# Four edits to a two-block transformer kernel: conv filling, PSUM rings, a fifth feed-forward weight buffer, and the place of weight splits in layer 1

## The chip, the cores and the metric

The kernel runs on one core of a Trainium2 chip. The metric is the device time of one execution in microseconds (us). Before the change three runs took 1944.5 to 1952.13 us, with a median of 1948.22.

## What is computed

Two model blocks follow each other, all in float32, with 256 latent tokens and 256 context tokens of width 1024. The first block has two layers:

```
layer 0: h += g1 * (concat(conv, neighbourhood attention) @ w_out)
         conv = gb * dwconv3(gc * u)          # gb, gc, u: columns of a @ w_in
         h += g2 * ((silu(n @ w1) * (n @ w3)) @ w2)    # D_FF = 2816
         the same for the context tokens
layer 1: window attention and differential attention, w_out
         mixture of 8 experts, top 2
```

The gates g1, g2 and the shifts and scales of the norms are `silu(c) @ ada_w + ada_b`. The second block has a dilated attention and a latent attention (q and kv go through norms of rank 512 and 256 and are projected up by `w_uq` and `w_ukv`), two sigmoid gates of 1024 columns each, `w_out`, and an MLP with squared ReLU.

## The kernel before

Every product of float32 data is made of three matmuls. An operand is split in a high part (rounded to the matmul's fp32r format) and a low part (what is left). Weights come from HBM in tiles of at most 128 x 2048 values (1 MB). A tile lands in the raw half of a buffer ("slot"). ScalarE writes the high part (line 1464, `whi`), then VectorE writes the low part over the raw values (line 1976, `wlo`). In the text this is the split. Then TensorE uses the tile (`mm3`, lines 889 to 891). In the trace each slot has three names: raw60, wlo61, whi62 for slot 0; raw64, wlo65, whi66 for slot 1; raw68, wlo69, whi70 for slot 2; raw137, wlo138, whi139 for the feed-forward's own slot. A smaller part of the slots' use is modulation: tiles of `ada_w` are not split but multiplied on VectorE with silu(c) and summed (line 2009, `wsum`), four instructions for two modulation vectors, two for one.

The order is fixed ahead. The five engines' programs are run once in Python to count semaphores and to lay out the tiles (`TILES`). `use` and `sums` give each tile the slot that has been out of use longest, from `open_slots`, or from `state["loads"]` and `state["adds"]` where these are set. SyncE issues the loads in one order and waits, for each, until the slot's previous tile is used up or summed. A modulation tile is loaded just after the weight tile that follows it. ScalarE and VectorE are strict in order as well. They call `feed(event)` ahead of nearly every operation. It splits all tiles up to the one in use at that event plus `at["ahead"]` (counted in tiles, modulation tiles too), and stops at a tile whose slot is still in use at that event. `feed` on VectorE also adds the sums that are owed.

PSUM has eight banks. `take(ring, ...)` goes around a list of banks (`RINGS`) and waits until the bank's last holder has been read. Rings "8", "4", "x", "c" are banks 0 to 7, 0 to 3, 0 to 3, and 4 and 5.

The places that the change touches, in the order of the run:

- Layer 0's attention ("a0", 32 units, from 157 us). Each step of the loop computes a unit's scores; the transposes and the product with V follow three and four units later. In between, TensorE works on a generator, here the 12 conv feature products (8 steps each of three matmuls; 96 steps in all). `FILLED[i]` says how many steps are done after unit i, `CONV_AT` in which unit each product ends, and ScalarE and VectorE take the results up in `convolved(i)`. 16 steps (the products c and u of the first feature group) are done before the attention, ahead of the transposes of the keys.
- Layer 0's feed-forward (366 to 766 us). Two blocks of 11 hidden tiles: 12 weight tiles of `w1` and `w3` by turns (48 matmuls each, the last two of a block 24), then `w2` in two halves of 3 tiles (48, 48 and 36 matmuls). 28 modulation tiles run beside them, one after each weight tile. The very last half goes token by token and so needs its three tiles at once. The results are multiplied by the gate on VectorE (line 2284) and added on GpSimd.
- Around the second block's last two halves ScalarE issues 13 small loads for layer 1 (lines 1667 to 1676), VectorE makes the rotation tables (`tables`, lines 2407 to 2416), and ScalarE then takes an exponential (line 1679).
- Layer 1: norm "o", projections cq (2 tiles) and ckv (1), then the pair tiles dq0, dq1, dk0, ..., and attention "a1" from 831 us.
- Second block: the last projections are the latents; their transposes, then the first products of the gates (two banks of eight, ahead of attention "a2"), then "a2" from 1557 us, and the products `uq` and `ukv` after it.

Of the kernel before, what the change touches and what calls it, by code (L numbers as in the profile page):

```python
# [280 lines left out]
def _build(nc, ctx, I, cst_d, scr_d, out_d, packed):  # L281
# [88 lines left out]
    HIDf = v3(LF.pair(11 * 512), 11)  # L370
    SILf, THDf = LF.some(3, 512), LF.some(3, 512)
    slot_f = slot(LF.col)
    LF.col += 4096
    slot_f_end = LF.col
    TMPf = LF.some(4, 512)
# [425 lines left out]
    FILLED = [16 + (i + 1) * 80 // 28 if i < 27 else 96 for i in range(40)]  # L801
    CONV_AT = {f: min(i for i in range(-1, 40) if ([16] + FILLED)[i + 1] >= 8 * (n + 1)) for n, f in enumerate(FEATS)}
    HEADS["a0"].filled = FILLED
    HEADS["a2"].filled = [min(64, 18 + 2 * i) for i in range(40)]
    GATE_AT = {(n, t): HEADS["a2"].filled.index(16 * n + 12 + 4 * t) if n else 0 for n in range(4) for t in range(2)}
# [16 lines left out]
    def tensor_program(e):  # L822
# [361 lines left out]
        for t in range(4):  # L1184
            if t == 0:
                fill = convolved()
                advance(fill, 16)
            head_turn(("k", t), XQ[t], 4, [("hn", "k", t)], "o")
        attend("a0", fill)
# [29 lines left out]
        if book.counting:  # L1219
            open_slots.remove(slot_f)  # L1220
# [158 lines left out]
        for g, (c0, w_) in enumerate(((2304, 512), (2816, 288))):  # L1379
            proj(("lat", g), x4(AT2s), 2, KT, w_in[:, c0:c0 + w_], w_, rdy("s"))  # L1380
            if g:
                for t in range(2):
                    head_turn(("lat", 0, t), XRs[(8 + t) % 3], 4, [("latn", 0, t)])
        fill = gates(x4(AT2s), w_in)
        advance(fill, 16)
        for t in range(2):
            head_turn(("lat", 1, t), XRs[(10 + t) % 3], 2, [("latn", 1, t)])
# [64 lines left out]
    def scalar_program(e):  # L1452
# [160 lines left out]
        for t in range(4):  # L1613
            at["ahead"] = 2 if t == 3 else 0
            head_hi("k", t, KT3)

        def convolved(i):
            for j in range(4):
# [6 lines left out]
                if i == CONV_AT["g", 3] + 1 + j:  # L1625
                    feed(("prod", "conv", "g", 3))
                    high("chi", (j,), YC[0][:, j, :], CV0[j], ("cv", j), ("prod", "conv", "g", 3))
        attend("a0", convolved)
        at["ahead"] = 2
        def norm_by_token(N, key):  # L1630
# [8 lines left out]
            at["ahead"] = 2  # L1639
# [6 lines left out]
        at["slots"].add(slot_f)  # L1646
        for blk in range(2):
            for f0 in range(0, 11, 2):
# [3 lines left out]
                for j in range(m):  # L1652
                    k = f0 + j
                    for s, n in due(("prod", "ff1", blk, f0, j), *(ff_free(blk, k, 3, "fth")), *normed_lo("f", 1)):
                        e.wait_ge(s, n)
# [211 lines left out]
        for t in range(2):  # L1867
            lat_hi(1, t)

        def gated(i):  # L1870
            for n_ in range(4):
                for t in range(2):
                    if i == GATE_AT[n_, t] + 1:
# [5 lines left out]
                        empties(("gate", n_, t), ("gcopy", n_, t))  # L1879
        attend("a2", gated)  # L1880
# [72 lines left out]
    def vector_program(e):  # L1953
# [385 lines left out]
        for t in range(4):  # L2339
            at["ahead"] = 2 if t == 3 else 0  # L2340
            l0_turned("k", t, KT3)

        def convolved(i):
            for j in range(4):
# [25 lines left out]
                if i == CONV_AT["g", 3] + 2 + j:  # L2370
                    feed(("prod", "conv", "g", 3))
                    low("clo", (j,), YC[1][:, j, :], cv, YC[0][:, j, :], ("chi", j))
        attend("a0", convolved)
# [19 lines left out]
        at["slots"].add(slot_f)  # L2393
# [24 lines left out]
        for blk in range(2):  # L2418
            for f0 in range(0, 11, 2):
# [3 lines left out]
                for j in range(m):  # L2423
                    k = f0 + j
                    th = THDf[(blk * 11 + k) % 3]
                    for s, n in due(("fsil", blk, k), ("prod", "ff3", blk, f0, j), *(ff_free(blk, k, 3, "fhl"))):
# [23 lines left out]
        at["ahead"] = 2  # L2450
# [98 lines left out]
        at["ahead"] = 1  # L2549
        for t in range(4):  # L2550
            feed(("prod", "od", "ckv", t))
        for t in range(2):
# [617 lines left out]
```

## Time and profile before

| | |
|---|---|
| median of 3 runs | 1948.22 us |
| the profiled execution | 1947.73 us |
| its span | 1945.8 us, mean granted TensorE clock 0.938 |
| TensorE busy | 1759.7 us, 90% of the span, 8958 matmuls |
| TensorE weight loads | 1473.3 us (they overlap) |
| VectorE busy | 1250.2 us, 64% |
| ScalarE busy | 824.3 us, 42% |
| GpSimd busy | 134.5 us, 7% |
| DMA | 332.59 MB, mean 171 GB/s |

Busy time is the union of an engine's instructions. In a timeline the idle time of the engine before an instruction stands in brackets, with what ended it.

### The profile page before, as it was taken

The numbers are of one execution on the slowest core, as the hardware profiler recorded it, in microseconds if no ns is written. First come the engines' busy times: TensorE is split into PE (matmuls) and PEld (weight loads), VectorE is DVE, ScalarE is ACT, GpSimd is POOL, SyncE is SP. The second block draws the span as 40 slices with busy tenths as digits, with TensorE's granted clock in tenths as the row PEclk, the third lists the DMA queues.
The fourth block names the chain that finished last, engine by engine and source line by source line (L and its number), as shares of the span: only waits on it lengthen the run. The fifth ranks groups of instructions, "written<-read, shape, count | busy, mean of one in ns | idle before, by whom it ended". The sixth has DMA issues, their size and how long they took to land. (4 is left out here: it accounts for less than half of the span.)

```text
span 1945.8 us, 22046 instructions
## 1 busy us (share of the span) xinstructions
PE 1759.7 (90%) x8958; PEld 1473.3 (76%) x8958; DVE 1250.2 (64%) x1709; ACT 824.3 (42%) x999; POOL 134.5 (7%) x128
## 2 busy tenths in 40 slices
PE   4896998899889997789879999999978998889998
PEld 2774786788677886689768888888868866769987
DVE  5455685468545553665758988888886645566643
ACT  5322232422212232333436777767745433445542
POOL 1230000200010001230010000000020000000000
PEclk8897997999989998889769999999999979998999
DMA  7431342255545441212137988888955511134553
GB/s 291 110 108 65 109 152 87 87 186 174 198 178 184 184 169 65 87 44 68 42 130 292 336 318 318 321 317 328 338 195 182 188 69 39 66 132 182 181 189 128
DMA packets 61436, 332.59 MB, mean 171 GB/s; under 512 B 16835, under 2 KB 17410, under 8 KB 28177
## 3 DMA queue, kind: packets, MB, share of 16 engines
q1 hardware_dynamic: 56080, 321.54, 45.7%
q10 hardware_dynamic: 4354, 6.32, 1.0%
q0 software_dynamic: 896, 3.26, 0.5%
q8 instruction: 74, 1.21, 0.2%
q14 instruction: 32, 0.26, 0.0%
HBM read 329.96 MB, written 1.13 MB: 170 GB/s over the span
## 5 line engine op out<-in xcount | busy, mean ns | idle before, releaser
L1976 DVE TENSOR_TENSOR wlo__65<-raw__64,whi__66 128x2048 fp32r<-128x2048 f32 (+2 forms) x68 | 157.0, 2308 | 115.4 <-ACT whi__66 L1464 115.4
L1464 ACT ACTIVATE whi__66<-raw__64 128x2048 fp32r<-128x2048 f32 (+2 forms) x68 | 127.0, 1868 | 119.0 <-DMA raw__64<-in_ffn_w 50.4
L1976 DVE TENSOR_TENSOR wlo__61<-raw__60,whi__62 128x2048 fp32r<-128x2048 f32 (+3 forms) x56 | 125.4, 2238 | 78.0 <-ACT whi__62 L1464 78.0
L1976 DVE TENSOR_TENSOR wlo__69<-raw__68,whi__70 128x2048 fp32r<-128x2048 f32 (+4 forms) x52 | 110.1, 2118 | 36.8 <-ACT whi__70 L1464 36.7
L1464 ACT ACTIVATE whi__62<-raw__60 128x2048 fp32r<-128x2048 f32 (+3 forms) x56 | 102.8, 1836 | 64.8 <-DMA raw__60<-in_ev_w_in 20.8
L2009 DVE SCALAR_TENSOR_TENSOR wsum__71<-raw__68,silu_rows 128x1024 f32<-128x1024 f32 x84 | 99.9, 1220 | 3.0 <-DMA raw__68<-in_ada_w 2.6
L1464 ACT ACTIVATE whi__70<-raw__68 128x2048 fp32r<-128x2048 f32 (+4 forms) x52 | 90.5, 1740 | 21.6 <-DMA raw__68<-in_w_ff 11.6
L2973 POOL TENSOR_TENSOR keep__58<-keep__58,keep__59 128x1 f32<-128x1 f32 (+3 forms) x48 | 49.2, 1026 | 634.8 <-DVE keep__58 L2048 634.8
L2231 DVE TENSOR_REDUCE keep__58<-ps 128x1 f32<-128x256 f32 (+1 forms) x104 | 56.6, 544 | 26.9 <-PE ps L891 20.1
L1464 ACT ACTIVATE whi__139<-raw__137 128x2048 fp32r<-128x2048 f32 (+2 forms) x15 | 26.2, 1744 | 108.1 <-DMA raw__137<-in_ffn_w 108.1
L1976 DVE TENSOR_TENSOR wlo__138<-raw__137,whi__139 128x2048 fp32r<-128x2048 f32 (+2 forms) x15 | 31.2, 2079 | 54.5 <-ACT whi__139 L1464 54.5
L889 PE MATMUL ps<-ffn__120,wlo__138 128*128 128x512 f32 x160 | 63.1, 395 | 2.5 <-issue 2.5
L889 PE MATMUL ps<-ffn__120,wlo__65 128*128 128x512 f32 x152 | 60.0, 395 | 3.4 <-issue 3.4
L890 PE MATMUL ps<-ffn__121,whi__139 128*128 128x512 f32 x160 | 62.8, 393 | 0.0
L891 PE MATMUL ps<-ffn__120,whi__139 128*128 128x512 f32 x160 | 62.8, 392 | 0.0
L890 PE MATMUL ps<-ffn__121,whi__66 128*128 128x512 f32 x152 | 59.9, 394 | 0.0
L891 PE MATMUL ps<-ffn__120,whi__66 128*128 128x512 f32 x152 | 59.7, 393 | 0.0
L1976 DVE TENSOR_TENSOR wlo__229<-raw__228,whi__230 128x2048 fp32r<-128x2048 f32 (+1 forms) x24 | 50.7, 2112 | 11.8 <-ACT whi__230 L1464 11.8
L1976 DVE TENSOR_TENSOR wlo__225<-raw__224,whi__226 128x2048 fp32r<-128x2048 f32 (+1 forms) x24 | 52.8, 2199 | 0.0
L2009 DVE SCALAR_TENSOR_TENSOR wsum__63<-raw__60,silu_rows 128x1024 f32<-128x1024 f32 x40 | 48.0, 1221 | 0.5
L1464 ACT ACTIVATE whi__226<-raw__224 128x2048 fp32r<-128x2048 f32 (+1 forms) x24 | 42.5, 1771 | 11.7 <-DMA raw__224<-in_moe_w 11.7
L1976 DVE TENSOR_TENSOR wlo__233<-raw__232,whi__234 128x2048 fp32r<-128x2048 f32 (+2 forms) x24 | 42.1, 1754 | 1.9 <-ACT whi__234 L1464 1.8
(1088 smaller groups left out, 5430.2 us busy)
## 6 DMA issues: line engine op xcount, KB each, us to landing
raw__68<-in_ada_w SPq DMA_DIRECT2D x26, 1024.0 KB, 5.0
raw__64<-in_moe_w SPq DMA_DIRECT2D x24, 1024.0 KB, 6.3
raw__60<-in_moe_w SPq DMA_DIRECT2D x24, 1024.0 KB, 6.3
raw__68<-in_moe_w SPq DMA_DIRECT2D x16, 1024.0 KB, 5.4
raw__224<-in_moe_w SPq DMA_DIRECT2D x16, 1024.0 KB, 5.0
raw__228<-in_moe_w SPq DMA_DIRECT2D x16, 1024.0 KB, 6.0
raw__60<-in_ada_w SPq DMA_DIRECT2D x15, 1024.0 KB, 6.3
raw__64<-in_ffn_w SPq DMA_DIRECT2D x13, 1024.0 KB, 4.9
```

Of the source, the lines that this page charges most:

```text
L889: e.matmul(out, ll, rh, start=start, stop=False)
L890: e.matmul(out, lh, rl, start=False, stop=False)
L891: return e.matmul(out, lh, rh, start=False, stop=stop)
L1464: e.activation(t.hi(), t.raw(), ACT.Copy).then_inc(*did("hi", i))
L1976: e.tensor_tensor(t.lo(), t.raw(), t.hi().bitcast(F32), ALU.subtract).then_inc(*did("lo", i))
L2009: m = e.scalar_tensor_tensor(out=junk, in0=slot_raw[t.slot][:, c * 1024:c * 1024 + 1024], scalar=1.0, in1=CB[:, v * D:(v + 1) * D], op0=AL ...
L2231: e.tensor_reduce(neg, b[:, 0:u.total], AX.X, ALU.max).then_inc(*link())
L2973: e.tensor_tensor(x, x, EXPO[:, 0:1].broadcast_to([128, n_]) if n_ > 1 else EXPO[:, 0:1], ALU.pow).then_inc(*did(out, *key))
```

## The change

The first edit spreads the conv filling over 31 units instead of 28, ends the first two conv products "before unit 0", and has ScalarE and VectorE take them up ahead of the key transposes' results (`convolved(-1)`). `HEADS["a0"].begun` stays 16, so the new `advance` line does nothing. The second edit gives the latents' transposes ring "x" instead of "8" and lets ScalarE copy the first two gate banks before the latents (`gated(-1)`). The third adds a second slot to the feed-forward (five in all), gives weights slots 0, 1 and `slot_f` and modulation tiles slot 2 and `slot_g`, and lays the residual's buffers `TMPf` on `SILf` and `THDf`; block 1's first Silu and product wait for block 0's last residual. The fourth sets `ahead` to 1 instead of 2 through norm "o" up to the cq projection's results, and to 2 instead of 1 at the feeds of ckv.

```diff
-    SILf, THDf = LF.some(3, 512), LF.some(3, 512)
-    slot_f = slot(LF.col)
-    LF.col += 4096
+    slot_f, slot_g = slot(LF.col), slot(LF.col + 4096)
+    LF.col += 8192
     slot_f_end = LF.col
-    TMPf = LF.some(4, 512)
+    SILf, THDf = LF.some(3, 512), LF.some(3, 512)
+    TMPf = SILf + THDf[0:1]
...
-    FILLED = [16 + (i + 1) * 80 // 28 if i < 27 else 96 for i in range(40)]
-    CONV_AT = {f: min(i for i in range(-1, 40) if ([16] + FILLED)[i + 1] >= 8 * (n + 1)) for n, f in enumerate(FEATS)}
-    HEADS["a0"].filled = FILLED
+    FILLED = [16 + (i + 1) * 80 // 31 if i < 30 else 96 for i in range(40)]
+    CONV_AT = {f: FILLED.index(min(x for x in FILLED if x >= 8 * n + 8)) if n > 1 else -2 for n, f in enumerate(FEATS)}
+    HEADS["a0"].filled, HEADS["a0"].begun = FILLED, 16
...
-    GATE_AT = {(n, t): HEADS["a2"].filled.index(16 * n + 12 + 4 * t) if n else 0 for n in range(4) for t in range(2)}
+    GATE_AT = {(n, t): HEADS["a2"].filled.index(16 * n + 12 + 4 * t) if n else -2 for n in range(4) for t in range(2)}
...
# tensor_program, feed-forward
                 if book.counting:
-                    open_slots.append(slot_f)
-                    lent[slot_f] = [("prod", "o", 0, 1, 3), ("res", ("o", 0), 1, 3)]
+                    open_slots.extend((slot_f, slot_g))
+                    lent.update({s: [("prod", "o", 0, 1, 3), ("res", ("o", 0), 1, 3)] for s in (slot_f, slot_g)})
+                    state.update(loads=(0, 1, slot_f), adds=(2, slot_g))
...
         if book.counting:
-            open_slots.remove(slot_f)
+            del open_slots[3:]
+        state.update(loads=None, adds=None)
...
# tensor_program, latents (both groups)
-                    head_turn(("lat", 0, t), XRs[(8 + t) % 3], 4, [("latn", 0, t)])
+                    head_turn(("lat", 0, t), XRs[(8 + t) % 3], 4, [("latn", 0, t)], "x")
...
# scalar_program; vector_program likewise (l0_turned for head_hi)
-        for t in range(4):
-            at["ahead"] = 2 if t == 3 else 0
-            head_hi("k", t, KT3)
-
         def convolved(i):
...
+        at["ahead"] = 1
+        convolved(-1)
+        for t in range(4):
+            at["ahead"] = 2 if t == 3 else 0
+            head_hi("k", t, KT3)
         attend("a0", convolved)
...
             norm_turned(N, 0)
-            at["ahead"] = 2
+            at["ahead"] = 1 if N == "o" else 2
...
                     for s, n in due(("prod", "ff1", blk, f0, j), *(ff_free(blk, k, 3, "fth")), *normed_lo("f", 1),
+                                    *([("res", ("ff2", 0), 1, 3)] if blk else [])):
...
         for t in range(2):
             odd_square("cq", t)
-        at["ahead"] = 1
+        at["ahead"] = 2
         for t in range(4):
             feed(("prod", "od", "ckv", t))
+        at["ahead"] = 1
...
-        for t in range(2):
-            lat_hi(1, t)
-
         def gated(i):
...
+        gated(-1)
+        for t in range(2):
+            lat_hi(1, t)
         attend("a2", gated)
# vector_program, after norm_turned("o", 0)
-        at["ahead"] = 2
         norm_scale("o", 3)
```

## Rows read from the trace of the kernel before

**Rows 1.** Windows: us, each engine's busy time (instructions), granted clock, DMA share, GB/s
```profile
419.40:430.40 11.00, 11.00 (x50) 9.12 (x49) 8.45 (x12) 3.56 (x4) 0.00 (x0) 1.00 0.55 191
200.00:297.00 97.00, 94.99 (x528) 76.35 (x527) 76.00 (x143) 29.96 (x64) 1.14 (x2) 1.00 0.34 120
297.00:318.00 21.00, 15.84 (x62) 12.51 (x62) 13.90 (x32) 6.97 (x18) 0.00 (x0) 0.50 0.41 150
1557.00:1577.00 20.00, 16.81 (x35) 10.04 (x36) 7.31 (x17) 6.73 (x13) 0.00 (x0) 0.50 0.04 17
```

**Rows 2.** The page's costliest groups (busy us, mean ns | idle) and its DMA issues
```profile
L1976 DVE TENSOR_TENSOR wlo__65<-raw__64,whi__66 128x2048 fp32r<-128x2048 f32 (+2 forms) x68 | 157.0, 2308 | 115.4 <-ACT whi__66 L1464 115.4
L1464 ACT ACTIVATE whi__66<-raw__64 128x2048 fp32r<-128x2048 f32 (+2 forms) x68 | 127.0, 1868 | 119.0 <-DMA raw__64<-in_ffn_w 50.4
L2009 DVE SCALAR_TENSOR_TENSOR wsum__71<-raw__68,silu_rows 128x1024 f32<-128x1024 f32 x84 | 99.9, 1220 | 3.0 <-DMA raw__68<-in_ada_w 2.6
...
raw__64<-in_ffn_w SPq DMA_DIRECT2D x13, 1024.0 KB, 4.9
```

**Rows 3.** Timeline of TensorE in the feed-forward: start, us, instruction [idle before]
```profile
513.49 0.47 PE L889 MATMUL ps<-whi__66,ffn__130 128*128 128x512 f32 x1 [2.87 <-DVE wlo__65 L1976]
...
539.17 0.80 PE L889 MATMUL ps<-whi__66,ffn__130 128*128 128x512 f32 x1 [6.35 <-DVE ffn__141 L2284]
...
573.56 0.76 PE L889 MATMUL ps<-ffn__120,wlo__138 128*128 128x512 f32 x1 [2.49 <-issue]
...
589.07 0.47 PE L889 MATMUL ps<-ffn__120,wlo__65 128*128 128x512 f32 x1 [2.75 <-issue]
...
739.10 0.77 PE L889 MATMUL ps<-whi__62,ffn__130 128*128 128x512 f32 x1 [3.95 <-DVE wlo__61 L1976]
```

**Rows 4.** Timeline of SyncE's loads in the feed-forward
```profile
575.90 0.33 SPq L3086 DMA_DIRECT2D raw__60<-in_ada_w  x1
576.27 0.43 SPq L3086 DMA_DIRECT2D raw__64<-in_ffn_w  x1
```

**Rows 5.** Timeline of ScalarE (small loads, exponential) and VectorE (tables) before layer 1
```profile
715.57 0.33 ACTq L1667 DMA_DIRECT2D odd__150<-in_od_cq_g  x1
...
720.29 0.45 ACTq L1672 DMA_DIRECT2D odd__149<-in_constants  x1
...
730.51 0.18 DVE L2407 SCALAR_TENSOR_TENSOR odd__154<-keep__49,odd__150 128x32 f32<-128x32 f32 x1
...
735.59 0.20 ACT L1679 ACTIVATE odd__156<-odd__156 128x2 f32<-128x2 f32 x1 [12.57 <-DVE odd__156 L2416]
```

**Rows 6.** DMA issues from 720 to 740 us: KB each, us to landing
```profile
raw__60<-in_ffn_w SPq DMA_DIRECT2D x1, 768.0 KB, 10.1
odd__149<-in_constants ACTq DMA_DIRECT2D x1, 256.0 KB, 7.2
```

**Rows 7.** Timeline of VectorE's splits in layer 1
```profile
768.45 2.29 DVE L1976 TENSOR_TENSOR wlo__69<-raw__68,whi__70 128x2048 fp32r<-128x2048 f32 x1 [4.81 <-ACT whi__70 L1464]
...
818.01 2.28 DVE L1976 TENSOR_TENSOR wlo__65<-raw__64,whi__66 128x2048 fp32r<-128x2048 f32 x1
820.21 2.29 DVE L1976 TENSOR_TENSOR wlo__61<-raw__60,whi__62 128x2048 fp32r<-128x2048 f32 x1
```

**Rows 8.** Timeline of TensorE in layer 1, up to its attention's first scores
```profile
773.78 0.76 PE L889 MATMUL ps<-whi__70,odd__169 128*128 128x512 f32 x1 [5.80 <-DVE odd__169 L2043]
...
820.44 0.55 PE L889 MATMUL ps<-whi__66,odd__169 128*128 128x256 f32 x1 [7.10 <-DVE wlo__65 L1976]
...
831.02 0.35 PE L889 MATMUL ps<-odd__164,odd__159 64*128 64x256 f32 x1 [1.36 <-DVE odd__165 L2043]
```

**Rows 9.** Timeline of TensorE and VectorE at the start of layer 0's attention
```profile
157.43 0.55 PE L889 MATMUL ps<-in__75,in__74 64*128 64x256 f32 x1 [8.28 <-ACT in__75 L1509]
...
159.27 0.75 DVE L2362 SCALAR_TENSOR_TENSOR in__80<-in__91,keep__51,in__80 128x512 f32<-128x512 f32 x1
```

**Rows 10.** Timeline of TensorE at the start of the dilated attention
```profile
1561.41 0.77 PE L889 MATMUL ps<-whi__259,mix__262 128*128 128x512 f32 x1 [2.79 <-ACT mix__241 L1877]
```

More of the change, by code:

```diff
@@ L370, in _build @@
     HIDf = v3(LF.pair(11 * 512), 11)
+    slot_f, slot_g = slot(LF.col), slot(LF.col + 4096)
+    LF.col += 8192
+    slot_f_end = LF.col
     SILf, THDf = LF.some(3, 512), LF.some(3, 512)
-    slot_f = slot(LF.col)
-    LF.col += 4096
-    slot_f_end = LF.col
-    TMPf = LF.some(4, 512)
+    TMPf = SILf + THDf[0:1]
+    assert LF.col <= CB0
     XSo = Region("odx", WORK + 4096).some(4, 1024)
@@ L1188, in tensor_program @@
             head_turn(("k", t), XQ[t], 4, [("hn", "k", t)], "o")
+        advance(fill, HEADS["a0"].begun - 16)
         attend("a0", fill)
@@ L1386, in tensor_program @@
         for t in range(2):
-            head_turn(("lat", 1, t), XRs[(10 + t) % 3], 2, [("latn", 1, t)])
+            head_turn(("lat", 1, t), XRs[(10 + t) % 3], 2, [("latn", 1, t)], "x")
         attend("a2", fill)
@@ L1645, in scalar_program @@
         norm_by_token("f", ("o", 0))
-        at["slots"].add(slot_f)
+        at["slots"].update((slot_f, slot_g))
         for blk in range(2):
@@ L1653, in scalar_program @@
                     k = f0 + j
-                    for s, n in due(("prod", "ff1", blk, f0, j), *(ff_free(blk, k, 3, "fth")), *normed_lo("f", 1)):
+                    for s, n in due(("prod", "ff1", blk, f0, j), *(ff_free(blk, k, 3, "fth")), *normed_lo("f", 1),
+                                    *([("res", ("ff2", 0), 1, 3)] if blk else [])):
                         e.wait_ge(s, n)
@@ L2338, in vector_program @@
         two = lambda x: x.rearrange("p (s t) -> p s t", s=2)
-        for t in range(4):
-            at["ahead"] = 2 if t == 3 else 0
-            l0_turned("k", t, KT3)
         def convolved(i):
@@ L2372, in convolved @@
                     low("clo", (j,), YC[1][:, j, :], cv, YC[0][:, j, :], ("chi", j))
+        at["ahead"] = 1
+        convolved(-1)
+        for t in range(4):
+            at["ahead"] = 2 if t == 3 else 0
+            l0_turned("k", t, KT3)
         attend("a0", convolved)
@@ L2392, in vector_program @@
         norm_turned("f", 1)
-        at["slots"].add(slot_f)
+        at["slots"].update((slot_f, slot_g))
         def tables():
@@ L2425, in vector_program @@
                     th = THDf[(blk * 11 + k) % 3]
-                    for s, n in due(("fsil", blk, k), ("prod", "ff3", blk, f0, j), *(ff_free(blk, k, 3, "fhl"))):
+                    for s, n in due(("fsil", blk, k), ("prod", "ff3", blk, f0, j), *(ff_free(blk, k, 3, "fhl")),
+                                    *([("res", ("ff2", 0), 1, 3)] if blk else [])):
                         e.wait_ge(s, n)
@@ L2548, in vector_program @@
             odd_rotate("cq", t)
-        at["ahead"] = 1
+        at["ahead"] = 2
         for t in range(4):
             feed(("prod", "od", "ckv", t))
+        at["ahead"] = 1
         for t in range(2):
```

## The prediction, made before the changed kernel ran

> **What bounds the kernel now.** I read the page first: TensorE is busy 90% of the span (the table ahead), so the time moves only where TensorE's idle time or its clock moves. Then the windows, which give the rate and the clock: a feed-forward tile of 48 matmuls is 11.0 us of unbroken work, and the first attention's middle is full (95 of 97 us busy, clock 1.00), while its tail and the start of the dilated attention run at 0.50, the 1.2 GHz level [rows 1]. Then the timeline of TensorE, for the idle time before single matmuls and who ended it, since all four parts touch such places. The rest of the path (experts, both mixers' other products, the final MLP) is not touched.
>
> The profiled execution took 1947.7 us (span 1945.8 and 1.9 around it), 0.5 under the median of 1948.2; I work against its trace and add the difference to the median.
>
> **Part A, the fifth feed-forward buffer.** Now four buffers serve weights and modulation tiles alike. By least recent use they settle so that weights alternate between raw64 and raw137 and modulation tiles between raw60 and raw68. So weight tile n+2 is loaded only when tile n is used up: 4.9 us load, 1.87 for ScalarE's half, 2.31 for VectorE's [rows 2], 9.1 in all. Beside a tile of 11 us that just fits; beside a tile of 36 matmuls (8.3 us) or 24 (5.5 us) it doesn't. The idle times show it: 2.87, 6.35, 2.49 and 2.75 us [rows 3]. The 2.49 and 2.75 are called "issue", but the load queue explains the second: the weight load waited in order behind a modulation load that VectorE's sums had to free, at 575.90 and 576.27, though its own buffer was free at 571.1 [rows 4].
>
> With three buffers for weights the 4.9 us leave the path and 4.2 us remain, under even a short tile. Place by place:
> - At 513.49 two sums of a modulation tile (each 4 x 1.22 us [rows 2], two modulation vectors in this stretch) stand ahead of the split on VectorE; these stay. I replay VectorE from the last feature tile: split, sum, split, sum, features, sum, split; it frees about 3 us, with the stall of the tile ahead of it (bounds 0 and 5.6).
> - The 6.35 us at 539.17 go: VectorE could not evict the first half's banks before it had split the tile ahead of it, which had to be loaded first. The next tile ran partly at the lower clock, as its first matmul of 0.80 us shows; I put 1.8 us on that: 8.1.
> - 2.49 and 2.75 go, each with about 1.7 us of lower clock: 8.6.
> - Against it, about 1.5 us of new late splits: early in the stage the third buffer's first use waits for a sum, and at the second block's third tile.
> Sum of these: 18 us gained, by about 590 us.
>
> Now the price. When the modulation tiles have run out, all four buffers go to weights today; after the change weights keep only three. The second of the three tiles of the last half then waits for the tile used up near 721.6 (today its buffer is free 11 us before). Its ScalarE half ran at 715.56, and the thirteen small loads of layer 1 stand behind it on ScalarE's queue [rows 5]. They start 11.0 us later. The masks among them landed 7.2 us after their issue at 720.29 [rows 5, 6], so at 738.5 instead of 727.5. VectorE's tables wait for them, ScalarE's exponential waits for the tables, and the last weight tile's two halves stand behind that. Today it takes 8.6 us from the tables' first operation at 730.51 to that matmul at 739.10, with the exponential at 735.59 between [rows 3, 5]. So that matmul comes at 738.5 + 8.6 = 747.1: an idle time of 12 us in place of 3.95, 8 us lost. The last tile itself is issued some 8 us later than now and needs as much as 10.1 us beside the small loads [rows 6], which lands it at 739.8, still in time. Bounds: 4 (small loads land faster) and 13. I take 9. Part A nets 9 us.
>
> In words of the Trainium skill (DMA: Bandwidth & Descriptors, Queues, rings and completion order) each DMA engine takes turns packet by packet between the queues it has work for; by that rule the moved loads slow the last weight tile as they do now. The rows agree: 768 KB took 10.1 us there, 1024 KB elsewhere 4.9. It speaks against this part, and the sum above holds it as measured.
>
> The feed-forward's residual buffers now lie on SILf and THDf, so the second block's first Silu waits for the last residual of the first block. GpSimd would be done some 2 us before that Silu's product. Behind the Silu stand only splits of a tile needed 10 us later. I count nothing; 0 to 2.
>
> **Part B, splits in layer 1.** (1) The first tile of layer 1's projection now goes to the buffer of the last modulation tile, free long before, and is split early. Today that split stands on VectorE at 768.45 to 770.74, ahead of the last eviction and of the norm [rows 7], and TensorE waits 5.80 us [rows 8]. Its products end at 766.2, so the norm starts 4.2 us earlier: 4.2. (2) The third tile's split leaves the second half of the norm, where its load ended it: about 1. (3) The product after the first two head projections waits 7.10 us for the split at 818.01 [rows 7, 8], behind the whole key chain on VectorE. After the change this split and the one before it (2 x 2.3 us) come ahead of that chain. VectorE passes the point after the split at 820.21 (ended 822.50) not sooner but 4.6 - 2.3 = 2.3 later, at 824.8; then four low halves, 1.4 us, and the attention begins at 826.2 instead of 831.02 [rows 8]: 4.8. TensorE itself waits some 1.7 us before the first pair tile, inside this. So the 7.1 us are not won, 4.3 to 4.8 are, as VectorE is late next. Part B: 9.5 us (bounds 4 and 14).
>
> **Part C, the conv filling.** Same matmuls, spread over 31 units, not 28. Ahead of unit 28 stand 88 of 96 steps instead of 96. A step is 3 matmuls, 3/48 of 11.0 = 0.69 us; eight are 5.5. Of these the first units' share is worthless: TensorE waits for VectorE there. Six to seven steps lie in the full stretch [rows 1]: 4.2 us. In the tail (297 to 318, 16 of 21 us busy at half clock [rows 1]) VectorE sets the pace with sums; its last conv steps move three units out, into its idle time: 1 us. Against this, the first feature's convolution now stands on VectorE before the key evictions: four steps, from 157.25 to the end of the last at 160.02, of which some 2.4 us weigh [rows 9]. TensorE idles there already (8.28 us [rows 9]), so all 2.4 us are on its path; but the same work leaves the place after the keys, and a sum and a split catch up by unit 4. I count 0, bounds 0 and 2.4. Part C: 5 us (1 to 9).
>
> **Part D, banks of the latents.** Counting takes around the rings, the latent transposes sit in banks 0 to 3 already, and ring "x" stands at bank 0 after 16 takes, so these banks stay. The next products (uq) move to 0 and 1, one of which the last output transpose still holds: 1 us lost. The gate's two copies move ahead of the latents: today TensorE waits 2.79 us for them at 1561.41 [rows 10]; their products are done by 1553.6 and ScalarE idles. That wait goes. Part D: 1.8, and 1.2 for the clock: 3 (0 to 9).
>
> For the clock: in the 20 us from 1557 it stands at 0.50 while TensorE is busy without a break from 1561.4 [rows 1, 10]. The shorter idle time may leave this as it is. By the Trainium skill (TensorE: Matmul & The Clock Gate, Part 1) the throttled state is the default and activity releases it; by that rule the full clock should come back soon after 1557.4. The row speaks against it, 15.6 us of work didn't release it. By the rule Part D would be 7 us more.
>
> **Sum.** 9 + 9.5 + 5 + 3 = 26.5; 1948.2 - 26.5 = 1921.7.
>
> **Rivals.**
> - *Part A's price isn't paid.* The small loads or the tables end early enough that the stall near 739 stays under 6 us, or the clock recovers sooner in D. For: the masks are 256 KB and today mingle with a weight load. Against: the order on ScalarE is fixed. Then 34 to 36 us: 1913. Chance 0.17.
> - *VectorE takes the gains back.* The freed time in the feed-forward turns into waits for splits behind sums (VectorE is busy 8.5 of 11.0 us per tile there [rows 1]), and Part C only moves the waits of the tail. Half of A's 18 and of C go: 26.5 - 11 = 15: 1933. Chance 0.22.
> - *Slower.* The price near 739 grows: layer 1's small loads run beside two weight loads (1.75 MB, not 0.75) and the masks land 10 us later still. Mechanism: every us of it goes straight to TensorE's idle time, and the clock stays low through the half (27 us of work, up to 13 lost). 18 - 8 - 10 - 13 = -13 for A, with B and C halved (+7) and D none: 1954. It decides from the point where the masks land 26 us later than now. Against: 1 MB takes 4.9 us. Chance 0.04; with other unforeseen collisions 0.06.
> - *No change*: C and D empty and A's gain halved, 8 us: 1940. Chance 0.10.
>
> **Numbers.** The forecast itself 0.45. About 0.5%, 9.7 us, is what a measurement can tell from none. Faster 0.82, same 0.12, slower 0.06. Range 1908 to 1941: below it more than the full gains of A, B and D's clock, above it half of everything lost.
>
> **What would show it.** Raw loads of weights cycling over three buffers and modulation tiles over two; no idle time over 1 us between the tiles of the first feed-forward block after the one near 510; the idle time before the last half's third tile near 12 us, with thirteen ScalarE loads starting near 708 (18 us earlier than 726.5); the wait of 7.10 gone and the layer 1 attention starting on VectorE's low halves; no wait on the gate copies. I am wrong if the 12 us stall is absent, if the stalls at 539 and 573 remain, or if the first attention ends less than 3 us earlier relative to its start.

## The result

The changed kernel takes 1923.01 us (median of 4, 1922.49 to 1925.34), the kernel before 1948.46 (median of 4): a ratio of 0.9878, 95% interval 0.9859 to 0.9897. The forecast was 1921.7 us. Run twice more, each time beside the kernel before on another chip, it gave 0.9869 (0.9848 to 0.9891) and 0.9865 (0.9842 to 0.9887).

The profiled execution took 1925.34 us, 2.3 over the median. Its page, the busy time first:

```profile
span 1923.5 us, 22047 instructions
PE 1751.9 (91%) x8958; PEld 1466.7 (76%) x8958; DVE 1250.8 (65%) x1709; ACT 824.2 (43%) x999; POOL 134.6 (7%) x128
```

The same 8958 matmuls; TensorE's busy time is 7.8 us shorter at a higher mean clock (0.943 against 0.938), and the rest of the 22.3 us is idle time. TensorE's timeline at the places of [rows 3] and [rows 8] shows the main exchange:

```profile
369.91 0.36 PE L890 MATMUL ps<-ffn__120,wlo__69 128*128 128x256 f32 x1 [2.43 <-DVE wlo__69 L1983]
...
427.45 0.47 PE L890 MATMUL ps<-ffn__120,wlo__132 128*128 128x512 f32 x1 [0.93 <-issue]
...
492.88 0.48 PE L890 MATMUL ps<-whi__66,ffn__130 128*128 128x512 f32 x1
...
506.83 0.77 PE L890 MATMUL ps<-whi__62,ffn__130 128*128 128x512 f32 x1 [2.81 <-DVE wlo__61 L1983]
...
527.54 0.39 PE L890 MATMUL ps<-whi__66,ffn__130 128*128 128x512 f32 x1
...
579.22 0.39 PE L890 MATMUL ps<-ffn__120,wlo__132 128*128 128x512 f32 x1
...
709.42 0.50 PE L890 MATMUL ps<-whi__66,ffn__130 128*128 128x512 f32 x1 [2.20 <-DVE ffn__140 L2291]
...
726.47 0.76 PE L890 MATMUL ps<-whi__133,ffn__130 128*128 128x512 f32 x1 [11.31 <-ACT whi__70 L1468]
...
757.16 0.47 PE L890 MATMUL ps<-whi__70,odd__169 128*128 128x512 f32 x1 [1.57 <-DVE odd__169 L2050]
...
766.44 0.76 PE L890 MATMUL ps<-whi__66,odd__169 128*128 128x512 f32 x1 [3.33 <-ACT whi__62 L1468]
...
809.19 0.35 PE L890 MATMUL ps<-odd__164,odd__159 64*128 64x256 f32 x1 [1.83 <-DVE odd__165 L2050]
```

In the kernel before, the matmuls that come here at 492.88 and 579.22 read:

```profile
499.50 0.47 PE L889 MATMUL ps<-whi__139,ffn__130 128*128 128x512 f32 x1 [2.68 <-DVE wlo__138 L1976]
...
601.69 0.39 PE L889 MATMUL ps<-ffn__120,wlo__138 128*128 128x512 f32 x1
```

The wait of 2.68 us is gone. The matmul of 539.17 comes at 527.54 without a wait; the waits of 2.49 and 2.75 us are gone, and no row stands for them. The third tile of the last half (739.10 before, now 726.47) waits 11.31 us instead of 3.95. The releaser printed there is a second split, of the next layer's tile, that ended at the same moment as the tile's own. SyncE's loads show the new cycle, weights over raw60, raw131 and raw64, modulation tiles over raw68 and raw135:

```profile
405.82 0.33 SPq L3095 DMA_DIRECT2D raw__60<-in_ffn_w  x1
406.58 0.33 SPq L3095 DMA_DIRECT2D raw__68<-in_ada_w  x1
406.97 0.42 SPq L3095 DMA_DIRECT2D raw__131<-in_ffn_w  x1
419.99 0.33 SPq L3095 DMA_DIRECT2D raw__135<-in_ada_w  x1
420.36 0.43 SPq L3095 DMA_DIRECT2D raw__64<-in_ffn_w  x1
```

The price of part A as ScalarE and VectorE show it (two timelines; before, these stood at 715.57, 720.29, 730.51 and 735.59 [rows 5]):

```profile
703.93 1.92 ACT L1468 ACTIVATE whi__62<-raw__60 128x2048 fp32r<-128x2048 f32 x1 [8.96 <-DMA raw__60<-in_ffn_w]
703.94 0.34 ACTq L1673 DMA_DIRECT2D odd__150<-in_od_cq_g  x1
...
711.10 0.46 ACTq L1678 DMA_DIRECT2D odd__149<-in_constants  x1
...
722.95 0.20 ACT L1685 ACTIVATE odd__156<-odd__156 128x2 f32<-128x2 f32 x1 [9.04 <-DVE odd__156 L2424]
723.06 1.47 ACT L1468 ACTIVATE whi__133<-raw__131 128x1536 fp32r<-128x1536 f32 x1
```

```profile
718.97 0.19 DVE L2415 SCALAR_TENSOR_TENSOR odd__154<-keep__49,odd__150 128x32 f32<-128x32 f32 x1 [7.49 <-DMA odd__149<-in_constants]
```

ScalarE splits the second tile only when its load has landed, the thirteen small loads follow, VectorE's first table operation is released by the masks, the exponential by the tables, and the last split by the exponential.

### The profile page after: what moved, and what is told of

Read it like the earlier page. It is cut to its first block and busy times, and to the rows that moved or that the text cites. A ratio compares the mean times of both kernels' runs of the same rounds, so it can differ in the third digit from the quotient of the medians.

```text
span 1923.5 us, 22047 instructions
## 1 busy us (share of the span) xinstructions
PE 1751.9 (91%) x8958; PEld 1466.7 (76%) x8958; DVE 1250.8 (65%) x1709; ACT 824.2 (43%) x999; POOL 134.6 (7%) x128
## 5 line engine op out<-in xcount | busy, mean ns | idle before, releaser
L1983 DVE TENSOR_TENSOR wlo__65<-raw__64,whi__66 128x2048 fp32r<-128x2048 f32 (+2 forms) x64 | 149.4, 2335 | 95.6 <-ACT whi__66 L1468 95.6
L1983 DVE TENSOR_TENSOR wlo__61<-raw__60,whi__62 128x2048 fp32r<-128x2048 f32 (+2 forms) x65 | 145.1, 2232 | 94.3 <-ACT whi__62 L1468 94.2
L1468 ACT ACTIVATE whi__62<-raw__60 128x2048 fp32r<-128x2048 f32 (+2 forms) x65 | 118.9, 1829 | 115.3 <-DMA raw__60<-in_ffn_w 62.7
L1468 ACT ACTIVATE whi__66<-raw__64 128x2048 fp32r<-128x2048 f32 (+2 forms) x64 | 120.7, 1886 | 102.7 <-DMA raw__64<-in_ffn_w 37.9
L2016 DVE SCALAR_TENSOR_TENSOR wsum__71<-raw__68,silu_rows 128x1024 f32<-128x1024 f32 x84 | 100.0, 1220 | 5.4 <-DMA raw__68<-in_ada_w 4.9
L890 PE MATMUL ps<-ffn__120,wlo__61 128*128 128x512 f32 (+1 forms) x128 | 46.9, 367 | 4.6 <-DVE ffn__121 L2050 3.3
L892 PE MATMUL ps<-ffn__120,whi__62 128*128 128x512 f32 (+1 forms) x128 | 46.4, 362 | 0.0
L891 PE MATMUL ps<-ffn__121,whi__62 128*128 128x512 f32 (+1 forms) x128 | 46.4, 362 | 0.0
L890 PE MATMUL ps<-ffn__120,wlo__132 128*128 128x512 f32 x112 | 43.7, 390 | 0.9 <-issue 0.9
L892 PE MATMUL ps<-ffn__120,whi__133 128*128 128x512 f32 x112 | 43.6, 389 | 0.0
L891 PE MATMUL ps<-ffn__121,whi__133 128*128 128x512 f32 x112 | 43.6, 389 | 0.0
L890 PE MATMUL ps<-ffn__120,wlo__65 128*128 128x512 f32 x112 | 43.6, 389 | 0.0
L891 PE MATMUL ps<-ffn__121,whi__66 128*128 128x512 f32 x112 | 43.6, 389 | 0.0
L892 PE MATMUL ps<-ffn__120,whi__66 128*128 128x512 f32 x112 | 43.6, 389 | 0.0
L2016 DVE SCALAR_TENSOR_TENSOR wsum__138<-raw__135,silu_rows 128x1024 f32<-128x1024 f32 x36 | 43.2, 1221 | 0.5
```

The costliest lines, as they stand in the source:

```text
L890: e.matmul(out, ll, rh, start=start, stop=False)
L891: e.matmul(out, lh, rl, start=False, stop=False)
L892: return e.matmul(out, lh, rh, start=False, stop=stop)
L1468: e.activation(t.hi(), t.raw(), ACT.Copy).then_inc(*did("hi", i))
L1983: e.tensor_tensor(t.lo(), t.raw(), t.hi().bitcast(F32), ALU.subtract).then_inc(*did("lo", i))
L2016: m = e.scalar_tensor_tensor(out=junk, in0=slot_raw[t.slot][:, c * 1024:c * 1024 + 1024], scalar=1.0, in1=CB[:, v * D:(v + 1) * D], op0=AL ...
```

## The stages, and how much the clock plays

This table is worked out from the traces: us between the same matmuls of each kernel, in brackets, for five of the stages, the part at the lower clock (0.50). "After" has three profiles of the same program; a_only to d_only are the kernel before with one of the four parts each (next section). A "score" is the first matmul of an attention.

| stage, from matmul to matmul | before | after, three profiles | a_only | b_only | c_only | d_only |
|---|---|---|---|---|---|---|
| start to first score of layer 0 | 157.4 | 158.8, 158.4, 158.4 | 156.2 | 157.1 | 159.6 | 157.2 |
| attention, to its output product | 160.5 (38) | 152.5 (26), 150.2 (24), 153.5 (31) | 160.1 (41) | 160.0 (41) | 149.3 (26) | 160.0 (41) |
| to the feed-forward's first tile | 48.5 | 49.3, 50.0, 48.6 | 49.5 | 48.6 | 49.4 | 48.6 |
| block 0 (to 573.56 of before) | 207.1 (10) | 196.9 (7), 194.7 (3), 193.1 (3) | 196.2 (7) | 207.2 (10) | 208.5 (11) | 207.1 (10) |
| to the last half's third tile | 165.5 (8.5) | 169.0 (8), 168.9 (8), 168.3 (8) | 168.9 (10) | 163.3 (3.3) | 163.4 (3.0) | 163.6 (3.4) |
| to layer 1's first product | 34.7 | 30.7, 30.7, 31.0 | 29.8 | 33.8 | 34.0 | 33.8 |
| to layer 1's attention | 57.2 | 52.0, 52.0, 52.1 | 58.1 | 50.6 | 57.2 | 56.9 |
| to the dilated attention | 726.3 (76) | 728.5 (82), 728.5 (82), 728.7 (82) | 728.3 (82) | 728.3 (82) | 728.2 (79) | 728.6 (82) |
| to the last matmul | 382.7 (47) | 380.2 (41), 380.1 (41), 380.1 (41) | 383.4 (48) | 376.8 (34) | 383.3 (48) | 380.3 (41) |

The fifth line shows what one profile is worth: b_only, c_only and d_only run there the code of before, and take 2 us less, because a stretch that stood at half clock in one execution did not in the others. The windows of the same 684 matmuls in the kernel before and in d_only, up to the third tile's wait (columns as in [rows 1]):

```profile
573.56:735.14 161.58, 158.83 (x684) 130.47 (x684) 89.72 (x138) 41.76 (x39) 10.23 (x8) 0.98 0.49 178
```
```profile
572.90:732.53 159.63, 157.16 (x684) 129.39 (x684) 89.73 (x138) 41.76 (x39) 10.23 (x8) 0.99 0.49 180
```

VectorE's and ScalarE's busy times agree to 0.01 us; TensorE's differs by 1.67 at a mean clock of 0.98 and 0.99. The last two lines show it as well. Up to the dilated attention this one profile of the kernel before took 2 us less than every other of the table, with 76 us at the lower clock instead of 79 to 82. And behind it b_only, with the code of before, took 6 to 7 us less than the kernel before, a_only and c_only, with 34 us at the lower clock instead of 47 or 48. So a part's worth is taken here from stages, with the unchanged kernels as the baseline, and whole times only as medians. The runs of one kernel on one chip spread by up to 13 us (x_both, below: 1902.84 to 1916.25).

## Experiments: each part alone

The four kernels are the kernel before with the hunks of one part. Their cores:

```diff
# a_only
-                    open_slots.append(slot_f)
+                    open_slots.extend((slot_f, slot_g))
+                    state.update(loads=(0, 1, slot_f), adds=(2, slot_g))
# b_only (norm "o" and the cq product; then the feeds of ckv)
-            at["ahead"] = 2
+            at["ahead"] = 1 if N == "o" else 2
...
-        at["ahead"] = 1
+        at["ahead"] = 2
# c_only
-    FILLED = [16 + (i + 1) * 80 // 28 if i < 27 else 96 for i in range(40)]
+    FILLED = [16 + (i + 1) * 80 // 31 if i < 30 else 96 for i in range(40)]
...
+        convolved(-1)
# d_only
-                    head_turn(("lat", 0, t), XRs[(8 + t) % 3], 4, [("latn", 0, t)])
+                    head_turn(("lat", 0, t), XRs[(8 + t) % 3], 4, [("latn", 0, t)], "x")
...
+        gated(-1)
```

**Part A.**

> Part A alone (five feed-forward buffers) on the kernel before. Both theories: the idle times of 6.35, 2.49 and 2.75 us go, some 18 us are gained by the middle of the second block, and the third tile of the last half waits 11 to 12 us for the exponential (3.95 before), which takes 8 to 10 us back. They differ on the first tile of layer 1. Theory 1 (as the prediction had it): its early split belongs to part B, so here TensorE still waits 5.8 us for the norm; 1948.5 - 9 = 1939.5 us. Theory 2: it is the buffer choice of part A that leaves slot 2 free for this tile, so the wait falls to 1.6 us here already; 1948.5 - 13.2 = 1935 us. Rival (VectorE takes the gains back): under 6 us gained, 1943 or more.

Measured: 1938.79 us against 1943.80 of the kernel before on that chip, ratio 0.9975 (0.9960 to 0.9989): 5 us gained (2 to 8). The timeline of TensorE in a_only:

```profile
730.79 0.76 PE L890 MATMUL ps<-whi__133,ffn__130 128*128 128x512 f32 x1 [9.64 <-ACT whi__70 L1467]
...
760.55 0.47 PE L890 MATMUL ps<-whi__70,odd__169 128*128 128x512 f32 x1 [1.57 <-DVE odd__169 L2047]
...
808.85 0.55 PE L890 MATMUL ps<-whi__66,odd__169 128*128 128x256 f32 x1 [7.08 <-DVE wlo__65 L1980]
```

Theory 2 holds: the wait of 5.80 us is 1.57 here. The last half's tiles no longer use slot 2, so layer 1's first tile lands there early. By stages, against the three kernels with the code of before, part A gives 11 us in block 0, pays 5.5 up to the third tile (where the 2.75 us that go are counted in), and gives 4 after it. It loses 1 ahead of block 0 and 1 in layer 1 (58.1 against some 57): 7.5 us. The median gives 5. The first term was expected at 18 us by the middle of the second block. From the feed-forward's first tile to the matmul of 601.69 a_only takes 217.9 us, the kernel before 235.3, b_only 233.2: 15 to 17.

**Part B.**

> Part B alone (how far ahead splits run in layer 1). Theory 1: all three steps of part B are its own: 4.2 + 1 + 4.3 to 4.8 = 9.5 us, 1939 us, and the wait of 5.80 us before layer 1's first tile falls to 1.6. Theory 2: the first step needs part A's buffers, the wait of 5.80 stays, and only 5 to 5.5 us are gained, 1943 us. Both: the wait of 7.10 us goes and VectorE's low halves start the attention some 4.5 us earlier relative to the layer's first product.

Measured: 1939.95 us, ratio 0.9978 (0.9963 to 0.9992), 4 us (2 to 7). TensorE in b_only:

```profile
770.07 0.76 PE L889 MATMUL ps<-whi__70,odd__169 128*128 128x512 f32 x1 [5.73 <-DVE odd__169 L2044]
...
812.13 0.28 PE L889 MATMUL ps<-whi__66,odd__169 128*128 128x256 f32 x1
...
820.64 0.35 PE L889 MATMUL ps<-odd__164,odd__159 64*128 64x256 f32 x1 [1.82 <-DVE odd__165 L2044]
```

Theory 2 again: the wait before the first product stays at 5.73, the wait of 7.10 is gone. From the first product to the attention it is 50.6 us in place of 57.2, 6.6 less; the full change takes 52.0, 5 less than before and 6 less than a_only.

**Part C.**

> Part C alone (conv filling over 31 units, first convolution ahead of the key results). The prediction's steps: 5 us (1 to 9), 1943.5 us. From the trace of all four together: 7 us gained at the end of the attention's tail, 2.7 of them lost again at the start of the feed-forward, where the second tile waits for its split (2.43 us in place of 0.97): 4.3 us net, 1944 us. Rival: the whole gain turns into waits of the feed-forward, which is paced by its loads here, and the time stays at 1948.

Measured: 1939.09 us, ratio 0.9974 (0.9960 to 0.9988), 5 us (2 to 8). By stages: 2.5 lost before the first score, 11 gained in the attention, 0.8 and 1.4 lost behind it: 6 us net. The rival is out. In the attention TensorE's idle time fell from 12.5 us (b_only and d_only) to 5.5, which is 7 of the 11 us. The other 4 are busy time (143.8 against 147.5), with 26 us at the lower clock instead of 41.

**Part D.**

> Part D alone (latents' transposes in ring x, the first two gate copies ahead of them). The prediction's steps: the wait of 2.79 us on the gate copies goes, 1 us is lost at the first latent product after the attention, 1.2 us from the clock: 3 us, 1945.5 us. From the trace of all four together the net may be 1 us: 1947.5 us. Rival by the clock rule: the full clock comes back at the start of the attention and 7 us more are gained: 1938 us.

Measured: 1944.38 us, ratio 1.0000 (0.9987 to 1.0013): nothing that the times show (2.5 us either way). By the stage table it gives 2.5 to 3 us from the dilated attention on, and here the traces are clear: all nine profiles of kernels with part D took 380 us in the last stage, without the wait of 2.79, and 17.1 us at the lower clock from the attention's start. Of the five without part D four took 382.7 to 383.4, with 20.5 us at the lower clock. The fifth is b_only. In the full change the matmul of [rows 10] and the first latent product read:

```profile
1538.76 0.79 PE L890 MATMUL ps<-whi__259,mix__262 128*128 128x512 f32 x1
...
1629.55 0.69 PE L890 MATMUL ps<-whi__66,mix__246 128*128 128x384 f32 x1 [0.93 <-DVE mix__273 L2050]
```

The wait of 2.79 is gone and 0.93 is lost, as forecast. The window shows the clock still down. Beside it stands the window of b_only, which has the code of the kernel before here:

```profile
1535.00:1555.00 20.00, 17.39 (x37) 10.26 (x37) 9.18 (x21) 6.17 (x12) 0.00 (x0) 0.57 0.15 53
```
```profile
1548.50:1568.50 20.00, 16.79 (x58) 10.39 (x58) 10.12 (x21) 9.37 (x17) 0.00 (x0) 0.83 0.19 68
```

In b_only the lower clock lasted 6.8 us from the attention's start, and the last stage took 376.8 us. So the 7 us of the rival exist in one execution of the fourteen profiled, and part D is not what brings them.

## Experiments: do the parts add up

The single parts gave 14 us (5, 4, 5 and 0; by their intervals 4 to 25) together where the full change gave 25. So it was run twice more, and parts A and B together.

> All four parts again, beside the others on one chip. The parts alone gave 4.9, 4.3, 5.1 and 0 us. Theory 1 (they add up, and the first comparison had a slow kernel before): 14 us, a ratio of 0.993. Theory 2 (part B's first step exists only with part A, or the parts help each other's clock): 20 us or more, a ratio of 0.990 or less.

Measured: 1921.15 us against 1949.53, ratio 0.9869 (0.9848 to 0.9891).

> All four parts, as the measure for the three others of this call. If the chip does not matter, a ratio of 0.987 to the kernel before, as on the two earlier occasions. If the smaller sum of the single parts (14 us) came from a faster kernel before on that chip, a ratio nearer 0.99 may come here.

Measured: 1920.87 us against 1946.37, ratio 0.9865 (0.9842 to 0.9887).

> Parts A and B together on the kernel before. Theory 1 (they add up as timed): 4.9 + 4.3 = 9 us, a ratio of 0.995. Theory 2 (the stages of the traces add up, which the clock's play hides in the single timings): 7.5 + 6.2 = 14 us, a ratio of 0.993. Both: the waits read 1.6 us before layer 1's first tile, about 10 to 11 us before the last half's third tile, and the wait of 7.10 is gone.

Measured: 1932.76 us, ratio 0.9926 (0.9910 to 0.9941): 14 us (11 to 18), theory 2's number. Its stages are those of a_only from the feed-forward's first tile to layer 1's first product (394.0 us against 394.9), and 52.2 us from there to the attention. In the traces the parts add up: 7.5 + 6.5 for A and B, with 6 for C and 2.5 to 3 for D some 23 us, where the spans differ by 22.3 to 26.5. Why the single parts timed less on their chip, whose kernel before was faster (1943.80), stays open. For A and B the two measurements don't contradict each other, as 4 to 15 and 11 to 18 us overlap. The changed kernel never ran on that chip, so that the whole change gives less there too is a rival that no run excludes.

## Experiments: the price of part A

Three edits of the changed kernel. x_early issues the thirteen small loads one tile sooner:

```diff
+            if blk:
+                at["ahead"] = 0
+                feed(("prod", "ff2", 1, 0, 0))
+                at["ahead"] = 2
+                ...   # the waits and the thirteen loads, moved here from below the loop
             for half in range(1 if blk else 2):
                 for t in range(4):
                     feed(("prod", "ff2", blk, half, t))
```

> The changed kernel, with ScalarE's thirteen small loads of layer 1 issued just behind the split of the last tile of block 1's first half (near 684 us), not behind the second tile of the last half (704 us). Theory 1 (the price of part A is the late masks, through tables and exponential): the masks land near 700, tables and exponential are done by 706, the third tile is split as soon as it has landed (712), and its wait falls from 11.3 to 1 to 3 us; 8 to 10 us gained, some 2 more by the clock: 10 us below the changed kernel. Theory 2 (the third tile's own late load is what counts): the wait stays over 6 us and less than 5 us are gained.

Measured: 1918.68 us against 1921.15 of the changed kernel on the same chip: 2.5 us. The masks left at 684.73; DMA issues, VectorE's and ScalarE's timeline and TensorE's:

```profile
odd__149<-in_constants ACTq DMA_DIRECT2D x1, 256.0 KB, 6.9
```
```profile
704.27 2.29 DVE L1987 TENSOR_TENSOR wlo__61<-raw__60,whi__62 128x2048 fp32r<-128x2048 f32 x1 [4.93 <-ACT whi__62 L1468]
706.48 0.68 DVE L2295 TENSOR_TENSOR ffn__139<-ps,keep__57 128x512 f32<-128x512 f32 x1
...
709.81 1.28 DVE L2419 SCALAR_TENSOR_TENSOR odd__154<-keep__49,odd__150 128x32 f32<-128x32 f32 x1
```
```profile
716.03 0.20 ACT L1689 ACTIVATE odd__156<-odd__156 128x2 f32<-128x2 f32 x1 [10.49 <-DVE odd__156 L2428]
```
```profile
719.55 0.76 PE L890 MATMUL ps<-whi__133,ffn__130 128*128 128x512 f32 x1 [6.00 <-ACT whi__70 L1468]
```

The masks were there at 684.73 + 6.9 = 691.6, and the tables began at 709.81 with nothing printed behind them. On VectorE they stood behind four evictions of the first half's results and the second tile's split, for whose high part VectorE had sat idle 4.93 us. Both theories missed this wait; the masks were the last releaser before, not the only one. The wait fell from 11.1 to 6.00, no further.

x_slot lets the last half use the modulation tiles' extra buffer:

```diff
                 by_token = blk and half
+                if by_token:
+                    state["loads"] = (0, 1, slot_f, slot_g)
```

> The changed kernel, with the three tiles of the last half allowed in the modulation tiles' extra buffer as well (slot_g), small loads as in the changed kernel. Every tile of the half is then loaded one step earlier. Theory 1: the small loads start near 697 us, masks land at 712, the exponential comes at 716, and the third tile's wait is some 5 us in place of 11.3: 6 us gained. Theory 2: with the third tile's load 8 us earlier the wait nearly goes (under 2 us), 9 us or more.

> Both edits: small loads early and the extra buffer for the last half. Both theories: no wait for the third tile (under 1 us), 11 us gained and 1 to 3 more by the clock: 12 to 14 us below the changed kernel. If x_early alone gives the same, theory 1 holds alone. Rival: VectorE or the clock takes it back and the gain is under 6 us.

Measured: x_slot 1910.84 us, 10.3 below the changed kernel on that chip; x_both 1909.38, 11.8 below (ratio to the kernel before 0.9793, 0.9770 to 0.9816). Both kept a wait, and the same one; in x_slot:

```profile
710.50 0.20 ACT L1687 ACTIVATE odd__156<-odd__156 128x2 f32<-128x2 f32 x1 [12.61 <-DVE odd__156 L2426]
```
```profile
714.01 0.77 PE L890 MATMUL ps<-whi__62,ffn__130 128*128 128x512 f32 x1 [3.94 <-ACT whi__70 L1470]
```

The tables' place on VectorE sets it, whether the small loads come early or not: in x_slot the masks landed at 702.5 and the tables began at 705.43, in x_both at 694.5 and 708.16, in both right behind the four evictions. The buffer did more than its 7 us of wait: the second tile's split now comes before the evictions, so the wait of 2.20 at 709.42 went too. The last kernel therefore moves the tables:

```diff
+            if blk:
+                at["ahead"] = 1
+                feed(("prod", "ff2", 1, 0, 0))
+                tables()
+                at["ahead"] = 2
             for half in range(2):
                 if blk and half:
                     ...
-                    tables()
```

> x_both, with VectorE's rotation tables moved ahead of the evictions of block 1's first half. In x_early and x_both the masks landed 18 us before the tables began, at 691 and 694: the tables stood behind these evictions, and the third tile waited 6.00 and 3.94 us for the exponential. Theory 1 (VectorE's order is the bound): tables run from 695 to 700, the exponential follows the split of the tile before, the third tile is split as soon as it lands (704), and its wait goes: 4 us by the wait and 1 to 2 by the clock, 16 to 18 us below the changed kernel. Theory 2 (the tables there delay the splits of the half's first two tiles): a wait of 3 us or more comes up at the first or second tile, and the total stays at x_both's 12 us.

Measured: 1908.43 us (1903.73 to 1909.37), 12.4 below the changed kernel on that chip, ratio to the kernel before 0.9797 (0.9780 to 0.9814). VectorE, ScalarE and TensorE in it:

```profile
693.78 0.19 DVE L2421 SCALAR_TENSOR_TENSOR odd__154<-keep__49,odd__150 128x32 f32<-128x32 f32 x1 [1.21 <-DMA odd__149<-in_constants]
...
697.45 0.29 DVE L2430 TENSOR_REDUCE odd__156<-odd__157 128x2 f32<-128x128 f32 x1
```
```profile
700.54 0.20 ACT L1691 ACTIVATE odd__156<-odd__156 128x2 f32<-128x2 f32 x1
702.57 1.49 ACT L1470 ACTIVATE whi__62<-raw__60 128x1536 fp32r<-128x1536 f32 x1 [1.82 <-DMA raw__60<-in_ffn_w]
```
```profile
711.81 0.39 PE L890 MATMUL ps<-whi__62,ffn__130 128*128 128x512 f32 x1
```

The last half has no wait left and never drops to the lower clock: 155.0 + 28.0 us on the two lines of the stage table where the changed kernel has 169.0 + 30.7. That is 16 to 17 us by the traces; the times give 12, no more than x_both's. Theory 1 has the mechanism and 4 us too many. In this profile block 0, whose code is the same, took 196.2 us, against 193.1 to 196.9 in the changed kernel's three profiles; whether the clock took the missing 4 us back in this or another way isn't shown. (The text above has the tables of x_both 18 us behind the masks; it was 14.) All its runs are faster than every run of the kernel before and of the changed kernel on its chip. It is not clearly faster than x_slot and x_both, which ran on another chip.

## Experiment: the convolution ahead of the key results

```diff
-        convolved(-1)
         for t in range(4):
             at["ahead"] = 2 if t == 3 else 0
             head_hi("k", t, KT3)        # on VectorE: l0_turned("k", t, KT3)
+        convolved(-1)
```

> The changed kernel, but with the first feature's convolution taken up behind the key results on ScalarE and VectorE, as it was before the change; the filling stays over 31 units. Theory 1 (this order costs): the two waits of 2.72 and 1.38 us at the key transposes go, the first score comes 1.5 to 2.4 us earlier, and the total is 1 to 2 us below the changed kernel. Theory 2 (the order pays): the work comes back behind the keys, TensorE waits 4 to 5 us near the first units' weighted sums again (4.64 at 187.6 in the kernel before), and the total is 1 to 2 us above.

Measured: 1918.58 us (1917.75 to 1920.29) against 1920.87 of the changed kernel (1915.98 to 1924.08) on the same chip. TensorE in the changed kernel, then in c_keys:

```profile
147.85 0.33 PE L896 MATMUL ps<-keep__49,in__79 128*128 128x128 f32 x1 [2.72 <-DVE in__78 L2325]
...
158.84 0.55 PE L890 MATMUL ps<-in__75,in__74 64*128 64x256 f32 x1 [7.82 <-ACT in__75 L1513]
```
```profile
146.07 0.33 PE L896 MATMUL ps<-keep__49,in__79 128*128 128x128 f32 x1 [0.41 <-DVE in__78 L2325]
...
157.06 0.55 PE L890 MATMUL ps<-in__75,in__74 64*128 64x256 f32 x1 [8.28 <-ACT in__75 L1513]
```

The first score comes 1.3 to 1.8 us earlier, and the wait of 4.64 at 187.6 does not come back (0.73 at 185.0, and 4.11 at 178.9 where the changed kernel has 3.83 at 180.70): the wider filling alone had removed it. The order costs about 1.5 us in the trace (theory 1), and the times lean that way, with ranges that overlap. Its attention took 147.7 us, with 11 at the lower clock, against 150.2 to 153.5 with 24 to 31; one profile can't say whether that belongs to the order.

## Why the prediction was right, step by step

- **Part A, the gain.** The step "18 us gained by about 590" held, term by term. From the feed-forward's first tile to the matmul of 601.69 the kernel before took 235.3 us (b_only, c_only and d_only 233.2 to 234.5), the changed kernel 218.6, 216.4 and 214.8: 15 to 20 us. The replay's 3 us "at 513, with the stall of the tile ahead of it" came at the tile ahead: its 2.68 us are gone, and 2.81 is left of 2.87 [rows 3]. The tiles behind the three other waits took 1.7 to 1.9 us more in the trace before, where 1.7 and 1.8 were counted. The late splits, "about 1.5", cost 0.7 to 0.9 (0.93 at 427.45). The rest of the spread is where a stretch of lower clock fell, at the tile behind 506.83 (1.5 us) and near 370. The wait of 2.43 at 369.91, 0.97 before, is nobody's: a_only and c_only have it too, b_only, d_only and one profile of the changed kernel do not. It is 0.94 where a stretch at half clock lies ahead of it and 2.4 where the stretch comes behind, and then the tile behind it is slow.
- **Part A, the price.** Forecast: an idle time of 12 us in place of 3.95, small loads 11 us later. Measured: 11.31 (11.1 and 10.7 in the other profiles), small loads from 703.94. Not forecast: 2.20 us at 709.42, where the late split of the second tile stands before the evictions that free its banks. "I take 9" held: 7.4 + 2.2 = 9.6.
- **Part B.** The sum held, the owner did not: step 1 (4.2 us, measured 5.80 - 1.57 = 4.23) is part A's, as a_only and b_only show. This link of the prediction's mechanism was wrong, and the total is right only because both parts were in the change. Steps 2 and 3 were forecast at 1 and 4.3 to 4.8; the stage lost 5.2. "The 7.1 us are not won" held: TensorE waits 1.83 us before the attention's first score in place of 1.36, and elsewhere for the VectorE work that moved ahead. Not forecast is the 3.33 us at 766.44, 1.39 before, for the split of the projection's second tile. It too is part A's: 3.33 in a_only, 1.59 in b_only.
- **Part C.** 5 us forecast, 4 to 8 by the stages, 5 by the median of c_only. The convolution's order, counted at 0 with bounds 0 and 2.4, costs about 1.5. The sum counted idle time alone. Of the 7 to 11 us that the attention lost, idle time is 7 in c_only and 3 to 5 in the changed kernel; the rest is less time at the lower clock, which no term had. That it came out near 5 net is in part luck.
- **Part D.** 3 us forecast, 2.5 to 3 in the traces, not resolved by the times; the "1.2 for the clock" was 3.4 us less at the lower clock. By the Trainium skill (TensorE: Matmul & The Clock Gate, Part 1) activity releases the lower clock, which would have made 7 us more. The window of 1535 to 1555 again doesn't bear it out: clock 0.57 with TensorE busy 17.4 of 20 us. The one of b_only does (0.83 with 16.8 busy), in the code of before, and its last stage is 6 to 7 us shorter. So the 7 us were right in size, but part D doesn't decide whether they come.
- **The masks.** I had them slow beside a weight load. They took 7.8 us in the changed kernel beside two weight loads and 6.9 in x_early, where the next weight load went out 1.9 us after them. What suffered there was that weight tile, of 1024 KB: issued at 686.60, it landed 8.5 us later, where 4.9 is usual [rows 2]. That fits the turns by packet in the Trainium skill (DMA: Bandwidth & Descriptors, Queues, rings and completion order), which I had applied to the last weight tile alone.

So the total was met by terms that mostly held: A's gain, its price, the third step of B and D. A's first tile was in the right sum under the wrong name. C's time at the lower clock was not foreseen, and neither were the waits of 3.33 and 2.43 us that took some of it back.

## What to carry to other kernels

A buffer taken from one stream is missed where that stream had run out: look at the last tiles, not the steady state, and lend the spare buffer back there (one line, 10 us here). In an engine that works in order, a wait that is removed shows the next instruction in the queue; before moving a load earlier, read what stands ahead of its consumer on the consumer's own engine. And do not attribute 2 us between two profiles before the same stretch of unchanged code agrees to better than that; here one such stretch differed by 6.

## What the runs showed of the hardware that I had not expected

The same 684 matmuls with nearly the same waits took 161.58 and 159.63 us in two executions, by a stretch of half clock that one had and the other had not; layer 0's attention had 24 to 31 us at half clock in the changed kernel and 11 in c_keys, and took 150.2 to 153.5 and 147.7 us. At the start of the dilated attention the lower clock lasted 20.5 us in four profiles without part D and 6.8 in the fifth, with the same code. A stretch at half clock costs less ahead of a wait that something else ends: 0.94 in place of 2.4 us of waiting near 370 is the time that it hides. In all fourteen profiles it is 9.3 us from the feed-forward's first tile to the next, with 3.4 us at half clock or with none. The time from there to the tile after it is 5.8 us at the full clock and 7.3 with the 3.4 us in it. A transfer of 256 KB needed 6.9 us with no weight load issued in the 9 us before it and one 1.9 us after it, more than 1024 KB does elsewhere (4.9); it had ten small loads just ahead of it in its own queue and two behind it. Whether these slowed it wasn't tried.
